# A seventh expert slot in a two-layer mixture-of-experts decoder kernel

## What is computed

```python
def hierarchical_moe(hn, w_group, b_group, w_router, b_router, w_gate, w_up, w_down):
    # top-1 of 4 groups, then top-2 of the 8 experts in it
    g_logits = t @ w_group + b_group
    ...
    for grp in range(N_GROUPS):
        a = jnp.einsum("nd,edf->nef", t, w_gate[grp])      # 1024 -> 256
        u = jnp.einsum("nd,edf->nef", t, w_up[grp])        # 1024 -> 256
        act = jax.nn.silu(a) * u * gates[:, grp, :, None]
        y = y + jnp.einsum("nef,efd->nd", act, w_down[grp])  # 256 -> 1024
```

## Time and profile before

| | us |
|---|---|
| median of 3 runs | 1150.63 (1149.26 to 1150.66) |
| the profiled execution | 1149.53 |
| its span, first to last instruction | 1147.7 |
| mean granted TensorE clock | 0.965 of full speed |

### The profile page before, as it was taken

The page is one execution under the profiler, slowest core; times in us unless marked ns, Lnnn a source line. Parts: engine busy times, 40 slices in busy tenths (PEclk is TensorE's granted clock), DMA queues, the critical chain, the costliest instruction groups (busy, mean ns, idle before and its releaser), DMA issues.

```text
span 1147.7 us, 13123 instructions
## 1 busy us (share of the span) xinstructions
PE 1029.5 (90%) x5160; PEld 549.3 (48%) x5160; DVE 402.8 (35%) x1115; ACT 255.2 (22%) x667; POOL 161.0 (14%) x170
## 2 busy tenths in 40 slices
PE   5999999999999999988838998989999999998890
PEld 3344644464455555444414647446455555554440
DVE  3122810362264322222234326458035432322225
ACT  3121710262121111000012226447012111110012
POOL 2000000001003333222111000000102233222210
PEclk9999999999999999999978999999999999998995
DMA  9610202215238999999978210023325999999975
GB/s 330 228 60 25 75 1 110 74 74 190 92 128 339 411 408 410 410 410 411 413 298 289 74 73 1 9 100 116 122 110 194 382 410 410 411 411 410 411 303 230
DMA packets 78814, 268.65 MB, mean 234 GB/s; under 512 B 13664, under 2 KB 17872, under 8 KB 69786
## 3 DMA queue, kind: packets, MB, share of 16 engines
q1 hardware_dynamic: 67056, 248.17, 55.3%
q0 software_dynamic: 11696, 19.62, 4.9%
HBM read 261.41 MB, written 23.10 MB: 248 GB/s over the span
## 4 chain that ended last, share of the span: by engine, by line
PE 71%; DMA 17%; DVE 5%; SPq 4%; ACT 2%; issue 1%; DVEq 0%; POOLq 0%; ACTq 0%
PE bank L735 13%; PE bank L951 12%; DMA W<-in_moe_w_up 10%; PE bank L825 10%; PE bank L747 9%; PE bank L964 7%; PE bank L766 5%; PE bank L777 2%; PE bank L940 2%; PE bank L793 2%; SPq L418 2%; DMA Q<-in_moe_w_up 2%; DMA oT<-in_moe_w_up 2%; PE bank L1071 2%; SPq L413 1%; PE bank L958 1%
## 5 line engine op out<-in xcount | busy, mean ns | idle before, releaser
L951 PE MATMUL bank<-W,K 128*64 128x256 f32 x768 | 186.1, 398 | 27.5 <-DMA W<-in_moe_w_up 25.7
L952 PE MATMUL bank<-W,K 128*64 128x256 f32 x768 | 186.2, 398 | 0.0
L951 PEld LDWEIGHTS bank<-W,K 128*64 128x64 f32 x768 | 105.6, 142 | 87.8 <-DMA W<-in_moe_w_up 29.5
L735 PE MATMUL bank<-hnT,W 128*128 128x512 f32 x336 | 145.1, 593 | 0.8 <-ACT hnT L1145 0.8
L1559 DVE SCALAR_TENSOR_TENSOR PT<-bank,V,PT 64x256 f32<-64x256 f32 x64 | 31.4, 490 | 273.8 <-ACT PT L1209 273.8
L952 PEld LDWEIGHTS bank<-W,K 128*64 128x64 f32 x768 | 105.6, 142 | 0.0
L735 PEld LDWEIGHTS bank<-hnT,W 128*128 128x128 f32 x336 | 63.5, 190 | 80.5 <-issue 79.5
L964 PE MATMUL bank<-D,PT 128*64 128x512 f32 x192 | 92.6, 604 | 0.7 <-ACT PT L1213 0.7
L966 PE MATMUL bank<-D,PT 128*64 128x512 f32 x192 | 92.6, 604 | 0.0
L587 POOL DMA_INDIRECT K<-rows,V x64 | 66.4, 1037 | 147.7 <-DVE V L1479 124.1
L1209 ACT ACTIVATE PT<-bank,V 64x256 f32<-64x256 f32 x64 | 29.9, 468 | 254.4 <-PE bank L952 251.8
(11 more groups left out here) (226 smaller groups left out, 1431.2 us busy)
## 6 DMA issues: line engine op xcount, KB each, us to landing
D<-in_moe_w_down SPq DMA_DIRECT2D x48, 1024.0 KB, 22.1
W<-in_moe_w_gate SPq DMA_DIRECT2D x48, 1024.0 KB
W<-in_moe_w_up SPq DMA_DIRECT2D x48, 1024.0 KB
hnT<-in_moe_w_down SPq DMA_DIRECT2D x16, 1024.0 KB, 21.7
W<-in_e_w_in SPq DMA_DIRECT2D x5, 2048.0 KB
Q<-in_moe_w_gate SPq DMA_DIRECT2D x8, 1024.0 KB
Q<-in_moe_w_up SPq DMA_DIRECT2D x8, 1024.0 KB
oT<-in_moe_w_gate SPq DMA_DIRECT2D x8, 1024.0 KB
```

Of the source, the lines that this page charges most:

```text
L735: last = nc.tensor.matmul(b[:, :], w[:, k, 128 * fb:128 * fb + 128], hnT[:, k, :], start=(k == 0), stop=(k == KD - 1))
L951: nc.tensor.matmul(bank[2 + e2][0:64, 0:256], xt, w[:, at:at + 256], start=first, stop=end)
L952: last = nc.tensor.matmul(bank[2 + e2][64:128, 0:256], xt, w[:, 2048 + at:2304 + at], start=first, stop=end)
```

## The change

The number of slots goes from six to seven. The seventh is made of `V` (gate), the first 2048 columns of `P` (up) and a new 8 KB tile `D4` (down). What lay in V moves: the router's tables go to a new tile `small`, two of the four `Y` buffers fall away, a one-partition list goes to a new tile `listed`. The router's transposed rows now go to two tiles of four 128 x 128 blocks, `rT`, one in `PT` and one in `V`, each used for all four chunks in turn; so `first_half` runs right before `second_half` of the same chunk, and ScalarE's order becomes squares, copy, root.

```diff
-    NSLOT = 6
-    SLOT_W = [("W2", "W3", "W0", "W1", "Q", "oT"), ("W2", "W3", "W1", "W0", "Q", "oT")]
-    SLOT_D = ("D0", "D1", "D3", "D2", "T1", "T0")
+    NSLOT = 7
+    SLOT_W = [("W2", "W3", "W0", "W1", "Q", "oT", "VP"), ("W2", "W3", "W1", "W0", "Q", "oT", "VP")]
+    SLOT_D = ("D0", "D1", "D3", "D2", "T1", "T0", "D4")
...
-        return e % NSLOT if e < 24 else (e - 24) % 4
+        return e % NSLOT if e < 21 else (e - 21) % 4
...
-        D = [sb(f"D{i}", [128, 2048]) for i in range(4)]
+        D = [sb(f"D{i}", [128, 2048]) for i in range(5)]
...
+        small = sb("small", [128, 520])
+        listed = sb("listed", [1, 480])
...
+        GATE_UP["VP"] = flatV, flatP[:, 0:2048]
...
-        Y = [flatV[:, 0:512], flatV[:, 512:1024], flatK[:, 3072:3584], flatK[:, 3584:4096]]
+        Y = [flatK[:, 3072:3584], flatK[:, 3584:4096]]
...
+        rT = [PT[:, 768:1280].rearrange("p (k t) -> p k t", k=4), flatV[:, 1536:2048].rearrange("p (k t) -> p k t", k=4)]
...
                 sp.wait_ge(s_og, 8 * lay + 8)
                 load_gate_up(lay, 5)
+                sp.wait_ge(s_sqrt, 8 * (lay + 1))
+                sp.wait_ge(s_lg, C * (lay + 1))
+                load_half(lay, 6, 0)
                 sp.wait_ge(s_g[0], 16 * (8 * lay + 1))
-                sp.wait_ge(s_lg, C * (lay + 1))
-                load_down(lay, 4)
-                load_down(lay, 5)
+                sp.wait_ge(s_ws, 2 * lay + 1)
+                sp.wait_ge(s_pfree, lay + 1)
+                load_half(lay, 6, 1)
...
-                for e in range(6, NE):
+                for e in range(NSLOT, NE):
...
-            load_down(0, 0)
-            load_down(0, 1)
+            for e in (0, 1, 6):
+                load_down(0, e)
...
             load_gate_up(0, 3)
+            load_down(0, 4)
+            load_down(0, 5)
             before_routing(0, ewout_v)
...
-            sp.wait_ge(s_gu, 24)
+            sp.wait_ge(s_gu, 20)
             load_cols("oT", odd_tile[0], owin_v, 0, 512)
-            sp.wait_ge(s_gu, 29)
+            sp.wait_ge(s_gu, 30)
...
-                        scatter(lay, Y[(e - 1) % 4], sidx[:, e - 1:e], s_sc[(e - 1) % 4])
-                    if e == 6:
+                        scatter(lay, Y[(e - 1) % 2], sidx[:, e - 1:e], s_sc[(e - 1) % 2])
+                    if e == 24:
                         pool.wait_ge(s_ncell, lay + 1)
+                        pool.wait_ge(s_gu, base + 21)
...
                         product(half, c, 0, 1)
-                        if half:
-                            if c:
-                                second_half(c - 1)
-                            else:
-                                first_half(3)
-                        elif c:
+                        if half and c:
                             first_half(c - 1)
+                            second_half(c - 1)
...
+                        if half and c == 3:
+                            first_half(3)
                         product(half, c, 4, 6)
...
-                    if base + e >= 4:
-                        dve.wait_ge(s_sc[e % 4], 16 * (8 * lay + e // 4))
-                    nc.vector.tensor_copy(Y[e % 4], bank[5 + e % 2][:, :]).then_inc(s_ye, 1)
+                    if base + e >= 2:
+                        dve.wait_ge(s_sc[e % 2], 16 * (16 * lay + e // 2))
+                    nc.vector.tensor_copy(Y[e % 2], bank[5 + e % 2][:, :]).then_inc(s_ye, 1)
...
-    nc = bacc.Bacc("TRN2", target_bir_lowering=False, num_devices=1)
+    nc = bacc.Bacc("TRN2", target_bir_lowering=False, num_devices=1, dynamic_dma_scratch_size=4096)
```

More of the change, by code:

```diff
@@ L362, in trunk @@
         s_ye = sem("down_out")
-        s_sc = [sem(f"rows_scattered{i}") for i in range(4)]
+        s_sc = [sem(f"rows_scattered{i}") for i in range(2)]
         ov = [{n: sem(f"further{l}_{n}") for n in
@@ L384, in expert_slot @@
             name = ("expert", NE * lay + e)
-            return BUF[w], BUF[d], landed(w, name), landed(d, name)
+            return GATE_UP[w], BUF[d], landed(w, name), landed(d, name)
         @block.sync
@@ L408, in load_expert, with load_half @@
                   .then_inc(down_done, 16)
+            def load_half(lay, e, part):
+                gate_up, _, done, _ = expert_slot(lay, e)
+                sp.dma_start(gate_up[part].rearrange("p (h x) -> p h x", h=2), (wg_v, wu_v)[part][lay][e])\
+                  .then_inc(done[0], 16 if slot_of(e) == 6 or not part else 32)
             def load_gate_up(lay, e):
-                gate_up, _, done, _ = expert_slot(lay, e)
-                for v, at, count in ((wg_v[lay], 0, 16), (wu_v[lay], 2048, 32)):
-                    sp.dma_start(gate_up[:, at:at + 2048].rearrange("p (h x) -> p h x", h=2), v[e])\
-                      .then_inc(done[0], count)
+                load_half(lay, e, 0)
+                load_half(lay, e, 1)
             def load_down(lay, e):
@@ L477, in load_expert_rows @@
             def load_expert_rows(lay):
-                for i in range(4):
-                    sp.wait_ge(s_sc[i], 16 * 8 * (lay + 1))
+                for i in range(2):
+                    sp.wait_ge(s_sc[i], 16 * 16 * (lay + 1))
                 y = y_dram[lay].rearrange("(s f) d -> s (f d)", f=4)
@@ L619, in expert_rows @@
                             pool.dma_start(krot_in, const_krot).then_inc(s_small, 16)
-                for s in range(4):
-                    pool.wait_ge(s_sc[s], 16 * 8 * (lay + 1))
+                for s in range(2):
+                    pool.wait_ge(s_sc[s], 16 * 16 * (lay + 1))
             def further_tiles(lay):
@@ L950, in gate_up @@
                         first, end = half + k == 0, half + k == 4
-                        nc.tensor.matmul(bank[2 + e2][0:64, 0:256], xt, w[:, at:at + 256], start=first, stop=end)
-                        last = nc.tensor.matmul(bank[2 + e2][64:128, 0:256], xt, w[:, 2048 + at:2304 + at],
+                        nc.tensor.matmul(bank[2 + e2][0:64, 0:256], xt, w[0][:, at:at + 256], start=first, stop=end)
+                        last = nc.tensor.matmul(bank[2 + e2][64:128, 0:256], xt, w[1][:, at:at + 256],
                                                 start=first, stop=end)
@@ L1496, in routing @@
                     for q, value in enumerate((wroot[:, k, :], rstd[:, 0:C])):
[L1497 to L1498 removed]
+                        nc.vector.tensor_tensor(wfacts[:, C * k:C * k + C, q, :], oh[k],
+                                                value.unsqueeze(2).to_broadcast([128, C, NE]), ALU.mult)
+                for k in range(2):
+                    then(nc.vector.tensor_tensor(epick, oh[k], iota.unsqueeze(1).to_broadcast([128, C, NE]), ALU.mult))
+                    ins = nc.vector.tensor_reduce(epos[k], epick, X, ALU.add)
+                    if k == 0:
+                        then(ins)
+                ins.then_inc(s_pfree, 1)
             def spread_ranks(lay):
@@ L1514, in records @@
                     nc.vector.tensor_copy(recv.bitcast(f32)[:, C * k:C * k + C, 3], rstd[:, 0:C])
-                for k in range(2):
-                    then(nc.vector.tensor_tensor(epick, oh[k], iota.unsqueeze(1).to_broadcast([128, C, NE]), ALU.mult))
-                    then(nc.vector.tensor_reduce(epos[k], epick, X, ALU.add))
+                dve.wait_ge(s_pfree, lay + 1)
                 for k in range(2):
```

130 lines of the change are left out of this document (66 added, 64 removed).

## The result

The changed kernel takes **1142.1 us** at the median (1140.23 to 1142.84, 4 runs), against 1150.56 of the kernel before in the same runs: ratio 0.9924, 95% interval 0.9909 to 0.9939. It is faster, by 8.4 us where the forecast had 14.6, and 1142.1 lies 0.1 us above the upper end of the range. The profiled execution took 1140.23 us (span 1138.3), 9.3 less than the one before.

A forecast was written before the change was run, and what follows sets the result against it. PE bounds the first part of each expert stage, weight loads at 410 GB/s the second. Stream -15.3 and first gather +1.2 sum to -14.1 us, 1135.4 on the profiled execution; forecast median 1136.0, range 1131 to 1142 us.

The forecast's parts named there:

- The bound: Expert stages: PE leads first, loads at 410 GB/s later; PE first late near expert 23, 500 us, up-load waits about halved.
- The stream, -15.3: Expert stages: one expert's loads fewer after the ring starts, 7.67 us a layer, 15.3 us saved in both.
- Expert 6's gate beside the first gather, +1.2: Start of each expert stage: the 1 MB gate load delays the first gather by 0.6 us a layer.
- the half clock only at the last expert: End of each expert stage: PE's slow clock after waits could add 2.4 us, up to 4.8 for both ends.
- my upper bound of 3.7: First gather of a stage: most it could be late per layer, landing in 6.8 us as under a full queue.
- My signs: Profile after: first gather 3 to 4.5 us, load after expert 0 at 352 to 353, layer 0's last up landing about 569.5.
- The router's rows, 0: Router and output projection: reordered transposes cost 0; no gain possible, at most 1.2 us a layer lost.
- DVE, two result buffers, loads in the attention, descriptor room: 0: Moved reductions, two result buffers for four and down loads moved into the attention cost 0; descriptor room not counted.
- Four slots from 21, 0: Late expert stage: four slots from expert 21 cost 0, the queue then holding over 18 us of transfers.
- The sum: Whole kernel: -15.3 + 1.2 = -14.1 us, 1135.4 on the profiled execution, 1136.0 forecast for the median.
- The forecast's case: Whole kernel: all terms stay within their bounds; chance 0.66.
- my first rival: Stage starts: first gathers land as under load, 6.8 to 10.3 us, eating the gain; 1141.6 to 1148.6 us, chance 0.12.

The follow-up runs named there:

- e1: The changed kernel with expert 6's gate load issued after the first gather has landed instead of before it; 1136.43 us, ratio 0.9863.
- e4: The changed kernel without its seventh slot: six slots, four from expert 24, the rest of the change kept; 1151.23 us, ratio 0.9986.
- e7: The changed kernel with the down loads of experts 4 and 5 moved from the attention to between expert 6's gate load and the first gather; 1147.40 us, ratio 0.9964.
- e11: The changed kernel with only expert 5's down load moved from the attention to between expert 6's gate load and the first gather; 1146.56 us, ratio 0.9946.
- e10: e1 with seven slots until expert 28 and four only for the last four experts, POOL's gain loads moved accordingly; 1133.60 us, ratio 0.9837.
- e12: The changed kernel with expert 6's gate load in the attention, e10's ring of slots and 256 more columns of filler before the transposes; 1132.54 us, ratio 0.9853.
- e3: e1 with six filler matmuls of 512 columns instead of four in front of the first gathered rows' transposes; 1137.33 us, ratio 0.9878.
- e9: The changed kernel with expert 6's gate load in the attention and expert 7's loads in halves, the first halves sent earlier; 1135.77 us, ratio 0.9850.
- e6: The changed kernel with expert 6's gate load held until the row indices are out, so issued together with the first gather; 1142.75 us, ratio 0.9925.

## Why the prediction was right in direction and 6 us off, point by point

*The bound.* Right. The loads set the second part of a stage at 410 GB/s. But PE falls behind them first at 519.43 us, not near 500, and its waits for up loads did not halve: 31.4 us before, 23.8 in the change. The late head is not the reason, for in e1, whose head is as short as before's in layer 0 (24.14 us), they are 23.2 us, the first at 516.76. Why they fell less than forecast is open.

*The stream, -15.3.* Right: -14.9, and e4 gives it back to 0.2 us.

*Expert 6's gate beside the first gather, +1.2.* This is the step that failed: the two heads cost +7.7. Two parts. The gather itself was late by 1.71 and 1.56 us, where I took 0.6, "near the lower end". I had counted on only a part of the megabyte being left when the gather's data start. But from the gather's issue to 346 us the engines still moved 376 GB/s x 3.43 us = 1.29 MB, of which the gather itself is at most 0.26:

```profile
342.57:346.00 3.43, 2.89 (x7) 0.95 (x5) 2.87 (x15) 0.22 (x2) 2.82 (x3) 1.00 0.95 376
```

And e7 and e11 show that the gather soon takes the 6.6 to 7 us of a full queue, with one extra load or with two. The second part I had nowhere in the sum. PE idles while it waits, its clock falls, and expert 0 takes 1.68 and 2.87 us longer. I had the half clock only at the last expert. Layer 1's 4.48 us lie beyond my upper bound of 3.7, for that reason. My signs said as much: the gather was to take 3 to 4.5 us (4.86 and 4.56), the load after expert 0 to go out at 352 to 353 (354.44), and the last up of layer 0 to land at 569.5 (PE starts on it at 571.6). e1 takes nearly all of both parts away with one moved line. Its 1136.4 us look like my number for the change, but its chip was slower; by the ratio it is 1134.8, which is 1.2 below my number.

*The router's rows, 0, "Below, no gain".* Wrong: there was a gain, and I had said there could be none. PE goes through the projection 1.15 us faster in each layer. The trace shows the gain and where it lies; that it comes from the transposes no longer standing between the first half's products is argued, not tried.

*DVE, two result buffers, loads in the attention, descriptor room: 0.* Right as far as e4 can tell. In the change DVE's copies into the two buffers wait for PE alone, all 64 of them, and never for a scatter; POOL's scatters wait for nothing but those copies and land within 7.4 us:

```profile
DVE K L1602 <- PE bank L975: 55.0, 64, 2.0
POOL expert_rows L603 <- DVE K L1602: 313.6, 64, 9.5
```

*Four slots from 21, 0.* Off by 0.5 to 1.5 us a layer, as the streams of e10 and e12 show; the queue was as full as I had said, so the reason is another one.

*The sum.* -14.9 + 7.7 - 0.9 - 1.3 = -9.4 of span. The last two terms, -2.2, are the router's rows (-1.15 a layer), +0.27 us by which the projection starts later in layer 0, and -0.18 between the stage's end and the projection in layer 1. That the time still came out at the edge of the range is in part luck: a gain that I had ruled out gave back 2.3 us of what the heads took. The forecast's case, all terms within their bounds, did not come about; the time lies where my first rival began (1141.6). The rival's place was right, the gather, but its size was not: it had 6.8 us or more to landing, and it was 4.9, with the clock as the rest.

## What to carry to other kernels

When a change puts a load ahead of a small transfer for which an engine waits, count the small transfer at up to its price in a full queue (6.7 us here, against 3 on idle engines), and then add what the waiting engine's clock does afterwards. Ask first whether the load has to go there: here nobody needed it for 50 us (expert 6's first matmul starts at 391.6), and moving it one line down was worth 7 us, half of what the seventh slot itself is. And find the event from which a bandwidth-bound stage really runs (here the end of expert 1); bytes moved out of the stretch before it are worth nothing.

## What the runs showed that I had not expected

PE's clock was low in other places in each profile, and the place decides the price. Over filler that has time to spare it costs nothing (in e1 338 to 341 us lie in it); over the last filler in front of the gather's transposes it cost 1.2 us or more (e3 and e9, layer 0); over expert 0 or 1 it costs about 1.5 us or more; in the second half of a stage the streams show no price (in the change the granted clock is 0.83 from 520 to 540 us). One place lies outside the experts. From the stage's end to expert 5's gate load in layer 1 the profiles of the changed kernels show 279.9 to 283.2 us. The two ends are e6 and e1, whose instructions are the same there. The timeline of 16 of PE's matmuls in e6, and in e1 the same 16 and a window, columns as before:

```profile
604.87 7.51 PE L760 MATMUL bank<-oT,hnT 128*128 128x512 f32 x16
```

```profile
599.87 9.20 PE L759 MATMUL bank<-oT,hnT 128*128 128x512 f32 x16
```

```profile
718.00:724.00 6.00, 5.13 (x31) 3.10 (x29) 2.66 (x10) 1.83 (x6) 0.59 (x1) 0.72 0.16 44
```

In e1 the low clock after the stage lasts longer into the next projection (1.7 us on these matmuls), and comes once more near 720 us, where e6 has full clock. That is over 3 us between two kernels whose code is the same there, more than most terms of this study, and the reason to compare heads and streams rather than times. Why the two differ was not tried.
